# First attention's order of steps rewritten: new sequence of products, earlier heads, roots one tick later, pooling beside other products, value banks swapped

## The reference

```python
h = rmsnorm(x, norm_attn_g)
u_q, u_k, u_v, u_pool, u_gate = split(h @ w_in)     # 1024, 1024, 1024, 512, 2048 columns
a = diff_attention(q, k, v, positions, lam, ...)    # 8 heads; each: rope on 16 of 64 dims, two causal
                                                    # softmaxes, w = p0 - lam * p1, o = w @ v, rmsnorm(o)
p = multiscale_pool(u_pool, w_pool, pool_scale)     # 4 groups: windowed mean minus input, @ w_pool
gates = sigmoid(u_gate)                             # two gates of width 1024
x = x + (gates[0] * a + gates[1] * p) @ w_out
```

## Time and profile before

| | |
|---|---|
| time, median of 3 | 1612.84 us (1612.76 to 1612.98) |
| profiled execution: its own time | 1608.91 us |
| profiled execution: span of the core | 1607.0 us |
| PE busy | 1577.4 us (98%) |
| DVE busy | 911.4 us (57%) |
| ACT busy | 634.2 us (39%) |
| granted clock of TensorE, mean | 0.997 |

### The profile page before, as it was taken

One profiled execution on the slowest core, in us unless ns is written; L12 is line 12 of the kernel. 1 busy time (PEld: TensorE's weight loads), 2 busy tenths in 40 slices (PEclk: granted clock), 3 DMA queues, 4 the chain that ended last, 5 costly groups with the idle time before them and its releaser, 6 DMA issues.

```text
span 1607.0 us, 18953 instructions
## 1 busy us (share of the span) xinstructions
PE 1577.4 (98%) x7352; PEld 1293.1 (80%) x7352; DVE 911.4 (57%) x1342; ACT 634.2 (39%) x988; POOL 80.6 (5%) x66
## 2 busy tenths in 40 slices
PE   8999989999999999999999999999999999999997
PEld 6777767788888888888778788888888888888886
DVE  6767766756654536347777545455555544434535
ACT  5445665643322213255444344344444322322313
POOL 3000000001000000031000010020002000000002
PEclk9999999999999999999999999999999999999999
DMA  5243222242333322323221133335223323333222
GB/s 201 83 118 93 82 73 75 69 149 89 103 105 92 104 92 92 105 84 104 79 77 62 59 115 103 111 104 159 66 79 105 100 97 96 101 96 100 93 85 73
DMA packets 49818, 155.70 MB, mean 97 GB/s; under 512 B 6209, under 2 KB 9281, under 8 KB 49601
## 3 DMA queue, kind: packets, MB, share of 16 engines
q1 hardware_dynamic: 49728, 154.49, 31.0%
HBM read 148.17 MB, written 2.10 MB: 94 GB/s over the span
## 4 chain that ended last, share of the span: by engine, by line
PE 93%; DVE 4%; ACT 2%; issue 1%; DMA 0%; SPq 0%; DVEq 0%; ACTq 0%
PE G L891 81%; PE SC L891 4%; PE TP L891 2%; PE O L891 2%; PE M L891 1%; DVE WL L1739 1%; ACT WH L1300 1%; PE TP L1212 1%; PE TP L1160 0%; PE M L1180 0%; DVE X L2244 0%; ACT T L1496 0%; DVE X L1785 0%; ACT L1297 0%; DVE XGl L1739 0%
## 5 line engine op out<-in xcount | busy, mean ns | idle before, releaser
L891 PE MATMUL G<-XGh,WH 128*128 128x512 f32 x1248 | 499.0, 400 | 2.3 <-DVE Vl L1740 2.2
L891 PE MATMUL G<-XGl,WH 128*128 128x512 f32 x1248 | 486.8, 390 | 0.0
L891 PE MATMUL G<-XGh,WL 128*128 128x512 f32 x1248 | 486.7, 390 | 0.0
L1739 DVE TENSOR_TENSOR WL<-RAW,WH 128x1024 fp32r<-128x1024 f32 (+3 forms) x281 | 338.6, 1206 | 183.1 <-ACT WH L1300 182.6
L1300 ACT ACTIVATE WH<-RAW 128x1024 fp32r<-128x1024 f32 (+3 forms) x281 | 283.7, 1011 | 179.6 <-PE G L891 171.9
L891 PEld LDWEIGHTS G<-XGh,WH 128*128 128x128 f32 x1248 | 234.6, 188 | 60.1 <-issue 8.4
L891 PEld LDWEIGHTS G<-XGh,WL 128*128 128x128 f32 x1248 | 234.6, 188 | 50.2
L891 PEld LDWEIGHTS G<-XGl,WH 128*128 128x128 f32 x1248 | 234.8, 188 | 48.1 <-issue 2.2
L891 PE MATMUL G<-MGh,WH 128*128 128x512 f32 x412 | 160.8, 390 | 1.0 <-ACT MGh L1300 0.6
L891 PE MATMUL G<-MGl,WH 128*128 128x512 f32 x412 | 160.4, 389 | 0.2 <-DVE MGl L1739 0.2
L891 PE MATMUL G<-MGh,WL 128*128 128x512 f32 x412 | 160.3, 389 | 0.0
(11 more groups left out here) (293 smaller groups left out, 1769.7 us busy)
## 6 DMA issues: line engine op xcount, KB each, us to landing
RAW<-in_up SPq DMA_DIRECT2D x32, 512.0 KB, 3.5
RAW<-in_dn SPq DMA_DIRECT2D x32, 512.0 KB, 3.5
RAW<-in_fg SPq DMA_DIRECT2D x22, 512.0 KB, 3.5
RAW<-in_fu SPq DMA_DIRECT2D x22, 512.0 KB, 3.5
RAW<-in_g SPq DMA_DIRECT2D x16, 512.0 KB, 3.5
RAW<-in_f SPq DMA_DIRECT2D x16, 512.0 KB, 3.5
X<-in_x SPq DMA_DIRECT2D x16, 256.0 KB, 4.3
RAW<-in_q SPq DMA_DIRECT2D x8, 512.0 KB, 3.6
```

The source lines that it names most:

```text
L891: return e.matmul(dst, st, mv, start=start, stop=stop, skip_group_check=True)
L1739: return e.tensor_tensor(dst, src, hi.bitcast(F32), ALU.subtract)
```

## The change

The list of steps of the first attention is written anew:

- **Order of products.** q and k of heads 4 to 7 come earlier, the gates and the pooling products later, and the two gates of a head can stand apart (`ORDER_A`).
- **Start of heads.** The first scores are planned when q0 to k2 are out (3 heads' q and k instead of 4), two ticks on: tick 23 instead of 25.
- **Roots.** `rs_a` is a tick behind `ss_a`; `op_a` moves a tick as well.
- **Pooling.** `wp` is two steps, `(i, 0)` ahead of the first half of the next product and `(i, 1)` ahead of its second; both write M, each followed at once by its `wp_out`.
- **Value banks.** Half 0 uses G0, G1, O, M; half 1 uses SC0, SC1, TP0, TP1, and its evictions stand in ticks 11 to 14. The sums of lambda, norm and columns ahead of them move to SC0, SC1, TP1.
- **Gates.** Gate 0 of head 6 goes to COS's tile and that of head 7 to X2 (`FREED_BY`).
- **Close.** Three `wo` products are begun ahead instead of two, the third in SC0, each with chunks 0 to 5 instead of 0 to 6.

```diff
-HEADS_A = [("qk", 0), ("qk", 1), ("qk", 2), ("qk", 3), ("pool", 0), ("gate", 0), ("qk", 4), ("wp", 0), ("pool", 1),
-           ("qk", 5), ("gate", 1), ("qk", 6), ("gate", 2), ("qk", 7), ("wp", 1), ("gate", 3), ("pool", 2), ("gate", 4),
-           ("wp", 2), ("pool", 3), ("gate", 5), ("gate", 6), ("wp", 3), ("gate", 7)]
-FIRST_A, PACE_A, BACKLOG = 4, 1.75, 6
+ORDER_A = ("q0 k0 q1 k1 q2 k2 q3 k3 u0 a0 b0 q4 k4 q5 k5 w0 u1 a1 b1 q6 k6 q7 k7 w1 a2 b2 u2 a3 b3 a4 u3 w2 b4 a5 b5 "
+           "a6 w3 b6 a7 b7")
+NAMES_A = {"q": "q", "k": "k", "a": "g0", "b": "g1", "u": "pool", "w": "wp"}
+FIRST_A, WAIT_A, PACE_A, BACKLOG = 6, 2, 1.75, 6
+SPARE = -1
+FREED_BY = {2: 0, 3: 1, 4: 2, 5: 3, 7: 4}
...
-CLOSING_A = (("pv_a", 6), ("sq_a", 7), ("ss_a", 8), ("rs_a", 8), ("op_a", 9))
+CLOSING_A = (("pv_a", 6), ("sq_a", 7), ("ss_a", 8), ("rs_a", 9), ("op_a", 10))
...
     def gemm(self, name, i, step):
         g = self.bank(step)
         self.tick()
+        beside, self.beside = self.beside, None
+        if beside is not None:
+            self.unit_of["wp", beside] = self.take("wp", beside, NW - 1)
+            self.pool_product(beside, 0)
...
         self.put("mm", u, g, 0)
         self.tick()
+        if beside is not None:
+            if beside > 0:
+                self.until("mix_y", 2 * beside - 1)
+                self.until("sum_a", 2 * beside - 1)
+            self.pool_product(beside, 1)
...
+    def pool_product(self, i, j):
+        self.put("wp", i, j)
+        self.put("wp_out", i, j)
+
+    def sums_soon(self):
+
+        return any(step[0] == "ss_a" for n in range(2) for step in self.jobs.get(self.clock + n, ()))
...
-        for m in range(3):
-            between.setdefault((3, m + 1), []).append(("vev", "va", 1, m))
         self.v_gemm("va", 1, 4, between)
-        self.put("vev", "va", 1, 3)
+        for m in range(4):
+            self.later(2 + m, "vev", "va", 1, m)
...
-                done = self.attention_a(self.clock)
+                done = self.attention_a(self.clock + WAIT_A)
...
-                if i > 0:
-                    self.until("mix_y", i - 1)
-                for w in range(2):
-                    if i > 1:
-                        self.until("sum_lo", i - 2)
...
+            elif kind == "g0":
+                if i in FREED_BY:
+                    self.until("mix_y", FREED_BY[i])
+                    self.until("sum_lo", FREED_BY[i])
+                self.gemm(kind, i, ("gate", i, 0))
+                self.later(0, "gate", i, 0)
+            elif kind == "g1":
+                if i > 0:
+                    self.until("mix_y", i - 1)
+                self.gemm(kind, i, ("gate", i, 1))
+                self.later(0, "gate", i, 1)
...
-        for n in range(2):
+        for n in range(3):
             step = ("residual", "wo", n)
-            g = self.bank(step)
+            g = self.bank(step) if n < 2 else SPARE
             self.tick()
             u = self.unit_of[step] = self.take("wo", n, NW - n)
             self.put("part", u, g, 0, 4)
             self.tick()
-            self.put("part", u, g, 4, 7)
+            self.put("part", u, g, 4, 6)
+        self.until("sum_lo", 6)
+        self.put("x1", 0)
         self.drain()
...
-            v_banks = {("va", 0): (SC[:, 0, :], SC[:, 1, :], TP[:, 0, :], TP[:, 1, :]),
-                       ("va", 1): (G[:, 0, :], G[:, 1, :], O[:, :], M[:, :]),
+            v_banks = {("va", 0): (G[:, 0, :], G[:, 1, :], O[:, :], M[:, :]),
+                       ("va", 1): (SC[:, 0, :], SC[:, 1, :], TP[:, 0, :], TP[:, 1, :]),
...
-            v_free = {("va", 1, 2): (lam_exp, 1), ("va", 1, 3): (col_done, COL["cols", "attn"]),
+            v_free = {("va", 1, 0): (lam_exp, 1), ("va", 1, 1): (ms_done, NRM["norm", "attn"]),
+                      ("va", 1, 3): (col_done, COL["cols", "attn"]),
...
```

More of the change, by code:

```diff
@@ L74, in plan @@
     for kind, i in HEADS_A:
[L75 to L80, removed]
+        u.append((kind, i, 256 if kind == "wp" else 1024))
     u += [("wo", n, 1024) for n in range(8)]
@@ L288, in heads_a @@
             if n == FIRST_A:
-                done = self.attention_a(self.clock)
-            if kind == "qk":
-                for w in range(2):
[L292 to L298, removed]
-                    self.rotate(i // 2)
-            elif kind == "gate":
+                done = self.attention_a(self.clock + WAIT_A)
+            if kind in ("q", "k"):
+                w = int(kind == "k")
+                self.gemm(kind, i, ("qk", i, w))
+                self.later(0, "qk", i, w)
+                if 2 * i + w < 3:
+                    self.later(0, "angles", 2 * i + w)
+                elif (i, w) == (1, 1):
+                    self.later(0, "sines")
+                if i % 2 == 1 and w == 1:
+                    self.rotate(i // 2)
+            elif kind == "g0":
[5 more added lines that the diff above has]
+            elif kind == "g1":
                 if i > 0:
                     self.until("mix_y", i - 1)
-                for w in range(2):
-                    if i > 1:
-                        self.until("sum_lo", i - 2)
-                    self.gemm(("g0", "g1")[w], i, ("gate", i, w))
-                    self.later(0, "gate", i, w)
+                self.gemm(kind, i, ("gate", i, 1))
+                self.later(0, "gate", i, 1)
                 gated[i] = self.clock
-                if ("wp", i // 2) in self.emitted:
+                if ("wp", i // 2, 1) in self.emitted:
                     self.chain(1, ("mix_y", i))
@@ L320, in heads_a @@
                 if i > 0:
-                    self.until("sum_a", 2 * i - 1)
-                self.tick()
-                while any(("ss_a", h) in self.emitted and ("rs_a", h) not in self.emitted for h in range(8)):
+                    self.until("mix_y", 2 * i - 2)
+                    self.until("sum_a", 2 * i - 2)
+                while self.sums_soon():
                     self.tick()
[L325 to L328, removed]
+                self.beside = i
                 for h in (2 * i, 2 * i + 1):
                     if h in gated:
-                        self.chain(1, ("mix_y", h))
-                        self.merge_a(h, max(done[h] + 1, self.clock + 2))
+                        self.chain(2 + h % 2, ("mix_y", h))
+                        self.merge_a(h, max(done[h] + 1, self.clock + 4))
     def residual(self, name, i, n, step):
@@ L353, in close_a @@
             step = ("residual", "wo", n)
-            if n < 2:
-                self.put("part", self.unit_of[step], self.turn_of[step], 7, 8)
+            if n < 3:
+                self.put("part", self.unit_of[step], self.turn_of.get(step, SPARE), 6, 8)
+                self.split_one()
                 self.put(*step)
@@ L644, in gate_of @@
         def gate_of(h, w):
-            return X[:, 3, :] if w == 1 else (X[:, 2, :], RB[:, :])[h % 2]
+            if w == 1:
+                return X[:, 3, :]
+            return {6: COS, 7: X[:, 2, :]}.get(h, (X[:, 2, :], RB[:, :])[h % 2])
         def pooled(h):
@@ L682, in turned_of, with norm_bank, cols_bank @@
             return ((WTh[:, :, :], WTl[:, :, :]), (QK[:, 0, 4:8, :], QK[:, 1, 4:8, :]))[c]
+        def norm_bank(name):
+            return SC[:, 1, :] if name == "attn" else M[:, :]
+        def cols_bank(name):
+            return TP[:, 1, :] if name == "attn" else M[:, :]
         def pm(h, m):
@@ L933, in made @@
                     return (mem_hi, k + 1), (mem_lo, k + 1)
-                if name == "wo" and i < 2:
+                if name == "wo" and i < 3:
                     return (mg_hi, MRH["sum_hi", k]), (mg_lo, MRL["sum_lo", k])
@@ L949, in g_bank, with m_bank @@
                     e.wait_ge(g_empty, EMPTY[freed_by[g - 2]])
+            def m_bank(step):
+                last = M_BEFORE[step]
+                if last is None:
+                    e.wait_ge(v_lo, VEV["vev", "va", 0, 3])
+                elif last[0] == "wp":
+                    e.wait_ge(y_done, WP[last])
+                else:
+                    e.wait_ge(ss_ln, POST[last])
             def chunks(u, g, k0, k1):
                 name, i, width = units[u]
-                dst = G[:, g % 2, 0:MEM] if name == "km" else G[:, g % 2, :]
+                dst = SC[:, 0, :] if g == SPARE else G[:, g % 2, 0:MEM] if name == "km" else G[:, g % 2, :]
                 if k0 == 0:
-                    g_bank(g)
+                    if g == SPARE:
+                        e.wait_ge(sa_max, 2 * SA["scores_a", 7, 3] - 1)
+                    else:
+                        g_bank(g)
                     e.wait_ge(w_hi, u + 1)
@@ L1074, in _ @@
                     e.wait_ge(d_one, 16)
-                    e.matmul(O[:, 0:2], ONE[0:HEAD, :], LP, start=True, stop=True).then_inc(lam_sum, 1)
+                    e.matmul(SC[:, 0, 0:2], ONE[0:HEAD, :], LP, start=True, stop=True).then_inc(lam_sum, 1)
                 elif kind == "norm":
@@ L1082, in _ @@
                     e.wait_ge(d_one, 16)
```

(55 more changed lines are left out.)

35 lines of the change are left out of this document (19 added, 16 removed).

## The result

The changed kernel takes 1601.37 us (median of 4, 1601.12 to 1602.64) against 1612.91 (median of 4): ratio 0.993, 95% interval 0.9913 to 0.9947. The forecast was 1606.7 with a range of 1602 to 1612, so the direction was right, and the time is 0.6 us under the range and 5.3 us under the likeliest value.

A forecast was written before the change was run, and what follows sets the result against it. TensorE was taken as the bound, so only its waits and slow clock could go: 14.4 - 6.2 - 1.3 - 0.8 = 6.1 us off the median 1612.84 gives 1606.7 us, range 1602 to 1612.

The forecast's parts named there:

- Value banks: At q0, after the values: G0 is emptied half of the values earlier, so TensorE's 2.2 us wait goes.
- First scores: At head 0's scores: TensorE arrives at 93.5, waits 4.5 us for the rotation's DMAs, plus 1.7 slow clock; 6.2 lost.
- Case B: Rival at the first rotation: DMAs land in 2.4 us and the clock holds; 1600.5 to 1603.5 us, chance 0.24.
- Middle: Between start and close: ScalarE waits for TensorE at eight `wp_out`, costing 1.3 us, from 0 to 2.6.
- C: Rival in the middle: waits move instead of going; 1615.8 us at most, half of it 1611, chance 0.22.
- D: Rival at M: it becomes the bound, eight waits of 2.4 us at wp and sums of squares; 1626 us, chance 0.08.
- idle time before the roots: On ScalarE, ahead of the roots' logarithm: idle time falls from 16.0 us to under 3.
- the empty ticks: Ticks 25 to 86: ten without half a product before, none after; aimed at waits at the scores, 7.9 us.
- Close: At the end of the first attention: waits of 0.3 for chunk 7 and 0.5 for G0; 0.8 us lost.
- the difference is carried over: Timed median 1612.84 was 3.9 us above the profiled execution; the forecast kept that difference on both sides.
- The 6.1: Whole kernel: net gain forecast, 14.4 us taken away less 6.2, 1.3 and 0.8 added.

The follow-up runs named there:

- e6: The kernel before with only the value banks swapped and their evictions spread; 1607.84 us, against 1612.64 for the kernel before beside it.
- e10: The changed kernel run again with no edit; 1600.96 us, against 1610.76 for the kernel before beside it.
- e2: The kernel before with only the roots and the scaling one tick later; 1602.41 us, against 1611.2 for the kernel before beside it.
- e0: The kernel before run again with no edit; 1613.0 us, against 1611.2 for the kernel before beside it.
- e8: The changed kernel with the sines a tick earlier and head 0's scores a tick later (24); 1600.63 us, against 1612.64 for the kernel before.

## Why the prediction was partly right, and where it failed

- **Value banks, right.** 2.2 us of wait forecast, 2.2 gone in e6, where no wait at the first products has come in its place. The gain between medians was larger, 4.8.
- **First scores, right as a mechanism.** Arrival forecast 93.5, measured 94.8 with a start 1.7 later and 93.2 in e10; wait forecast 4.5, measured 5.5 and 4.4 in two profiles, with a slow clock behind in both. Case B fell: the last of the DMAs needed 5.3 us, not 2.4.
- **Middle, mis-sized.** I took 1.3 us for ScalarE's new idle time at `wp_out`. No wait shows for it, neither at the scores nor at M. C and D fell with it. The idle time before the roots went to 2.6 us, as forecast. But the empty ticks, to which I gave a share of the 4.2 us wait, left only 1.5 us of it once the roots were late (e2).
- **Close, right.** 0.8 forecast, 0.5 measured.
- **What failed: "the difference is carried over".** I read one profiled execution, saw that it was 3.9 us faster than the runs beside it, and moved that 3.9 to both sides. It was no constant. The profiled execution had a slow clock after one of its waits; that of e0 has it after three (6.8 us in all), with the same waits. The change removes those waits and so that cost too: the gain between the medians was 11.5 us. With the 3.9 counted as removed the forecast would have been 1602.8.
- **The 6.1 itself, in part luck.** Between the two profiled executions the difference was 6.3. But from 6.1, the later start takes 1.7, the longer wait at the first scores 1.0 and the slow clock behind it 0.1 (3.6 x 0.50 = 1.8 against 1.7), while the middle gives 1.3 back and the close 0.3. That makes 4.9; the other 1.4 or so stand in no wait of the profile, and where they were gained stays open.

Why the first tile of x comes 1.7 us later in some executions was not studied, nor was any experiment made that fixes whether a given wait is followed by the slow clock.

## What to carry to other kernels

Where one engine is the bound and the profiled execution is faster than the timed ones, compare granted clocks before carrying the difference over: short waits of TensorE can each cost about as much again in slow clock (0.34 x 5 = 1.7 us behind one of 1.4, 0.35 x 3.6 = 1.3 behind one of 2.2), in some executions only, and that goes together with the wait. Undo the parts of a large change one by one: here one number (a root behind its sum by a tick) and a swap of banks gave 1.9 us more than the whole change; the pooling, gates and close gave 2.7 on top, and the new sequence with its earlier start took 4.6 back. When a chain has a fixed length, moving its start trades the wait at one end for one at the other; a shorter chain (a faster pace) removes both.

## What the runs showed of the hardware

- The same program took 1608.7 to 1614.1 us over its executions, at mean granted clocks of 0.997 down to 0.993; two profiled ones, 4.7 us apart, had the same waits. Fewer waits do not always mean less spread: it was 0.5 us with roots alone (e2), but 4.4 in e8.
- A wait of 2.2 us was followed by a clock of 1.00 in one execution and of 0.65 over 3.6 us in another; one of 1.4 us by 1.00 and by 0.66 over 5 us.
- Four DMAs of 128 KB between on-chip tiles landed in 2.4 us (median) by themselves and in up to 5.3 us with loads of 512 KB issued around them.
